# Attention steps between the gate and branch products of the merge, and merged tiles in two of four weight buffers

## What is computed

```python
hn = rms_norm(x, norm_mix[l])
proj = jnp.einsum('bsd,dn->bsn', hn, w_in[l])
p_rwkv, p_pool, p_att, p_gate = jnp.split(proj, split_at, axis=-1)
...
y_a, v_first = rwkv7_bidir(p_rwkv, hn, vres, v_first, ...)
y_b = multiscale_pool(p_pool, pool_w[l], pool_scale[l])
y_c = gqa_axial(p_att, q_norm[l], k_norm[l])
gates = jax.nn.sigmoid(p_gate).reshape(B, S, N_BRANCH, D)
merged = (gates[:, :, 0] * (y_a @ w_branch_rwkv[l]) + gates[:, :, 1] * (y_b @ w_branch_pool[l])
          + gates[:, :, 2] * (y_c @ w_branch_attn[l]))
x = x + merged @ w_out[l]
x = x + expert_choice_ffn(rms_norm(x, norm_ffn[l]), router[l], exp_gate[l], exp_up[l], exp_down[l])
```

## Time and profile before

| | us |
|---|---|
| median of 3 runs | 3319.7 |
| lowest and highest run | 3315.34, 3321.82 |
| span of the profiled execution, first to last instruction | 3318.4 |
| TensorE busy in it | 3219.3 (97%) |
| VectorE busy | 1527.3 (46%) |
| ScalarE busy | 1068.0 (32%) |
| GpSimd busy | 308.7 (9%) |

### The profile page before, as it was taken

One profiled execution on the slowest core, in us unless ns is written; L12 is line 12 of the kernel. 1 busy time (PEld: TensorE's weight loads), 2 busy tenths in 40 slices (PEclk: granted clock), 3 DMA queues, 4 the chain that ended last, 5 costly groups with the idle time before them and its releaser, 6 DMA issues. The chain is left out here.

```text
span 3318.4 us, 46903 instructions
## 1 busy us (share of the span) xinstructions
PE 3219.3 (97%) x20286; PEld 2468.8 (74%) x20286; DVE 1527.3 (46%) x2217; ACT 1068.0 (32%) x1596; POOL 308.7 (9%) x365
## 2 busy tenths in 40 slices
PE   9999999999999999999999999979999999989988
PEld 7888887888888888889788888758877888434332
DVE  5443556644435544332754434685567544201112
ACT  4222226432224322222732223553344323200001
POOL 1000131200001000000300001211111301100000
PEclk9999999999999999999999999989999999999999
DMA  4222441122233222332222222301010323899998
GB/s 144 102 90 90 145 143 40 39 102 89 90 96 113 102 89 90 96 107 108 84 97 94 98 88 98 106 20 49 3 65 20 105 99 124 345 427 425 425 427 336
DMA packets 62799, 448.77 MB, mean 135 GB/s; under 512 B 8705, under 2 KB 10369, under 8 KB 32641
## 3 DMA queue, kind: packets, MB, share of 16 engines
q1 hardware_dynamic: 62592, 445.76, 35.9%
HBM read 438.39 MB, written 2.10 MB: 133 GB/s over the span
## 5 line engine op out<-in xcount | busy, mean ns | idle before, releaser
L569 DVE TENSOR_TENSOR w_lo<-slot,w_hi 128x2048 fp32r<-128x2048 f32 (+4 forms) x243 | 487.1, 2005 | 331.6 <-ACT w_hi L560 329.3
L167 PE MATMUL bank<-xa,w_hi 128*128 128x512 f32 x1368 | 535.9, 392 | 1.2 <-DVE w_lo L3170 1.1
L168 PE MATMUL bank<-xa,w_hi 128*128 128x512 f32 x1368 | 532.4, 389 | 0.0
L169 PE MATMUL bank<-xa,w_lo 128*128 128x512 f32 x1368 | 532.3, 389 | 0.0
L560 ACT ACTIVATE w_hi<-slot 128x2048 fp32r<-128x2048 f32 (+4 forms) x243 | 406.1, 1671 | 335.5 <-PE bank L169 326.3
L167 PE MATMUL bank<-xb,w_hi 128*128 128x512 f32 x832 | 324.7, 390 | 0.7 <-DVE w_lo L569 0.6
L168 PE MATMUL bank<-xb,w_hi 128*128 128x512 f32 x832 | 323.7, 389 | 0.0
L169 PE MATMUL bank<-xb,w_lo 128*128 128x512 f32 x832 | 323.7, 389 | 0.0
L167 PEld LDWEIGHTS bank<-xa,w_hi 128*128 128x128 f32 x1368 | 256.8, 188 | 63.1 <-issue 5.4
L169 PEld LDWEIGHTS bank<-xa,w_lo 128*128 128x128 f32 x1368 | 256.8, 188 | 53.8
L168 PEld LDWEIGHTS bank<-xa,w_hi 128*128 128x128 f32 x1368 | 256.8, 188 | 53.4 <-issue 1.2
(11 more groups left out here) (511 smaller groups left out, 4872.4 us busy)
## 6 DMA issues: line engine op xcount, KB each, us to landing
slot<-in_w_gu SPq DMA_DIRECT2D x87, 1024.0 KB, 4.7
slot<-in_exp_gate SPq DMA_DIRECT2D x25, 2048.0 KB, 15.2
slot<-in_exp_up SPq DMA_DIRECT2D x24, 2048.0 KB, 15.0
slot<-in_exp_down SPq DMA_DIRECT2D x24, 2048.0 KB, 15.8
slot<-in_w_dn SPq DMA_DIRECT2D x64, 704.0 KB, 4.0
slot<-in_w_gate SPq DMA_DIRECT2D x24, 768.0 KB, 4.3
xe<-in_exp_up SPq DMA_DIRECT2D x8, 2048.0 KB, 13.4
xe<-in_exp_down SPq DMA_DIRECT2D x8, 2048.0 KB, 15.2
```

The costliest lines, as they stand in the source:

```text
L167: e.matmul(out, w[0], x[0], start=(j == 0), stop=False)
L168: e.matmul(out, w[0], x[1], start=False, stop=False)
L169: return e.matmul(out, w[1], x[0], start=False, stop=(j == n - 1))
L569: dve.e.tensor_tensor(lo, slot(k, b), hi.bitcast(F32), ALU.subtract).then_inc(L.up("w_lo", b))
```

## The change

The attention of stage `ax` no longer runs ahead of the merge. `pe_attention`, `act_attention` and `dve_attention` take a function `between(t)` that is called at the end of each step, and the merge hands them 20 pieces, one for each step (`AX_PIECES`): the gate and the branch product of the first branch for all 8 tiles in turn, then gate (0, 1), the pool mix, branch (0, 1) and gate (0, 2). The other products come after the attention (`AX_REST`). The weight blocks are reordered to match: first the 8 blocks of branch 0, then tile by tile those of branches 1 and 2. The split of `y_rwkv` into `yr` moves ahead of the attention. ScalarE and VectorE take up a piece one step after TensorE, and split a weight block in every second step.

Memory: `yr` now lies where the attention doesn't use memory; six of the eight tiles `mg` lie in buffers 2 and 3, so that all weights of the merge and of the output product go through buffers 0 and 1, and the first expert block (buffers 2 and 3) waits for the last split tile, `("mg_lo", 7)`.

```diff
+    late_mg = Arena(k.nc, SBUF_END - SLOT - 1024, a.made)
+    m.mg = [late_mg.buf(512, "mg") for _ in range(6)] + [k.sq[1], k.sqsum]
...
-    add("w2_gate", [ins["w2_gate"][m, z] for m in range(KT) for z in range(3)], 1536)
+    add("w2_gate", [ins["w2_gate"][m, 0] for m in range(KT)] + [ins["w2_gate"][m, z] for m in range(KT) for z in (1, 2)], 1536)
...
-        if b == k.first["w2_gate"] + 6:
-            slots = [2] + slots
+        if b == k.first["w2_gate"]:
+            slots.remove(3)
+        if b == k.first["exp"]:
+            slots = [2, 3] + sorted(slots)
+            held[2] = held[3] = ("mg_lo", 7)
...
+AX_PIECES = [(kind, i, 0) for i in range(KT) for kind in ("gate", "branch")] + [("gate", 0, 1), ("mix", 0, 1), ("branch", 0, 1), ("gate", 0, 2)]
+AX_REST = [("branch", 0, 2)] + [(kind, i, z) for i in range(1, KT) for z in (1, 2) for kind in ("gate", "branch")]
...
+    def between(t):
+        if t < len(AX_PIECES):
+            piece(*AX_PIECES[t])
+
+    pe_attention(k, "ax", k.ax.att, ax_units(k), between)
+    for name in AX_REST:
+        piece(*name)
     pe_out(k, "mg", nx, k.first["w2_out"], m.out, lambda i: ("mg_lo", i))
...
+    def between(t):
+        if 0 < t <= len(AX_PIECES):
+            kind, i, z = AX_PIECES[t - 1]
+            if kind == "gate":
+                sigmoid(i, z)
+            if kind == "mix":
+                act_pool_mix(k)
+        if t < 18 and t % 2 == 0:
+            act_weight(k, k.first["w2_gate"] + t // 2 + 1)
+        if t == 19:
+            act_weight(k, gate_block(k, 1, 1))
+
+    act.wait_ge(*L.at("rwkv_out", 3))
+    act.wait_ge(*L.at("z_mean", 3))
     for j in range(4):
         e.activation(m.yr[j][0], col(k.y_rwkv, j), ACT.Copy).then_inc(L.up("yr_hi", j))
+    act_attention(k, "ax", k.ax.att, ax_units(k), between)
```

More of the change, by code:

```diff
@@ L386, in plan_memory @@
     assert b.at <= first_dead.at
-    b = first_dead.copy()
-    late_mg = [b.buf(512, "mg") for _ in range(4)]
+    b = Arena(k.nc, first_dead.at + 2048, a.made)
+    yr_hi, yr_lo = b.copy(), z.copy()
+    m.yr = [(yr_hi.buf(512, "yr", F32R), yr_lo.buf(512, "yr", F32R)) for _ in range(4)]
     k.y_pool = [b.pair("y_pool") for _ in range(4)]
-    m.yr = [b.pair("yr") for _ in range(4)]
-    m.mg = [b.buf(512, "mg") for _ in range(4)] + late_mg
+    late_mg = Arena(k.nc, SBUF_END - SLOT - 1024, a.made)
+    m.mg = [late_mg.buf(512, "mg") for _ in range(6)] + [k.sq[1], k.sqsum]
+    b.at = first_dead.at + 12288
     m.out = [(b.buf(512, "mg_out", F32R), Arena(k.nc, rstd8_at, a.made).buf(512, "mg_out", F32R))] + k.xs[1:]
@@ L856, in width, with pe_attention @@
     return math.prod(keys.shape[1:])
-def pe_attention(k, st, m, units):
+def pe_attention(k, st, m, units, between=None):
     pe, e, L = k.pe, k.pe.e, k.led
@@ L910, in pe_attention, with act_attention @@
                 last.then_inc(L.up("scores", st, t, z))
-def act_attention(k, st, m, units):
+        if between:
+            between(t)
+def act_attention(k, st, m, units, between=None):
     act, e, L = k.act, k.act.e, k.led
@@ L956, in pool_attention, with dve_attention @@
         pool.e.tensor_tensor(out[1], m.ot[s % 3], out[0].bitcast(F32), ALU.subtract).then_inc(L.up("att_out", st, s))
-def dve_attention(k, st, m, units):
+def dve_attention(k, st, m, units, between=None):
     dve, e, L = k.dve, k.dve.e, k.led
@@ L1645, in pe_post @@
     pe_values(k, "ax", 0, k.first["w2_attv"], 128, k.xs, tok)
-    pe_attention(k, "ax", x.att, ax_units(k))
 def by_chunks(b, soon):
@@ L1781, in act_post @@
             L.up("v_out", "ax", 0, i))
-    act.wait_ge(*L.at("rwkv_out", 3))
-    act_attention(k, "ax", x.att, ax_units(k))
 def dve_shift(k, n):
@@ L2016, in dve_post @@
     dve_weight(k, b["w2_gate"])
-    dve_attention(k, "ax", x.att, ax_units(k))
 def pool_rwkv(k):
@@ L2545, in sp_ax, with gate_block, gate_turn @@
         c += n
+def gate_block(k, i, z):
+    return k.first["w2_gate"] + (KT + 2 * i + z - 1 if z else i)
+def gate_turn(i, z):
+    return KT + 2 * i + z - 1 if z else i
+AX_PIECES = [(kind, i, 0) for i in range(KT) for kind in ("gate", "branch")] + [("gate", 0, 1), ("mix", 0, 1), ("branch", 0, 1), ("gate", 0, 2)]
+AX_REST = [("branch", 0, 2)] + [(kind, i, z) for i in range(1, KT) for z in (1, 2) for kind in ("gate", "branch")]
 def pe_merge(k, nx):
@@ L2550, in pe_merge, with piece @@
     ys = [(m.yr, lambda j: ("yr_lo", j)), (k.y_pool, lambda j: ("ypool_lo", j)), (k.y_att, lambda j: ("att_out", "ax", 4 * j + 3))]
[L2551 to L2554, removed]
+    def piece(kind, i, z):
+        if kind == "mix":
+            pe_pool_mix(k)
+            return
+        b = gate_block(k, i, z)
+        w = views(part(k, b), "p (k c) -> p k c", k=12)
+        if kind == "gate":
             pe.wait_ge(*L.at("w_lo", b))
@@ L2560, in pe_merge @@
             last.then_inc(L.up("gate2", i, z))
-            if i == z == 0:
-                pe_pool_mix(k)
+        else:
             bank, freed = k.banks.take(("branch", i, z), ("branch_gated", i, z))
@@ L2574, in act_merge, with sigmoid @@
     act, e, L, m = k.act, k.act.e, k.led, k.mg
-    act.wait_ge(*L.at("att_out", "ax", 15))
+    def sigmoid(i, z):
+        sg = m.sgs[gate_turn(i, z) % 3]
+        act.wait_ge(*L.at("gate2_scaled", i, z))
+        e.activation(sg, sg, ACT.Sigmoid).then_inc(L.up("gate2_sigmoid", i, z))
+    def between(t):
+        if 0 < t <= len(AX_PIECES):
+            kind, i, z = AX_PIECES[t - 1]
+            if kind == "gate":
+                sigmoid(i, z)
+            if kind == "mix":
+                act_pool_mix(k)
[5 more added lines that the diff above has]
+    act.wait_ge(*L.at("z_mean", 3))
     for j in range(4):
         e.activation(m.yr[j][0], col(k.y_rwkv, j), ACT.Copy).then_inc(L.up("yr_hi", j))
[L2578 to L2585, removed]
+    act_attention(k, "ax", k.ax.att, ax_units(k), between)
+    for i in range(1, KT):
+        for z in (1, 2):
+            act_weight(k, gate_block(k, i, z) + 1)
+            sigmoid(i, z)
         if i == 3:
@@ L2597, in dve_merge @@
     dve, e, L, m = k.dve, k.dve.e, k.led, k.mg
-    for j in range(4):
-        dve.wait_ge(*L.at("yr_hi", j))
-        e.tensor_tensor(m.yr[j][1], col(k.y_rwkv, j), m.yr[j][0].bitcast(F32), ALU.subtract).then_inc(L.up("yr_lo", j))
     def split(i):
@@ L2603, in split, with scaled @@
         e.tensor_tensor(m.out[i][1], m.mg[i], m.out[i][0].bitcast(F32), ALU.subtract).then_inc(L.up("mg_lo", i))
[L2605 to L2614, removed]
-                dve_pool_mix(k)
-            if t == 3 * KT - 1:
+    def scaled(i, z):
+        t = gate_turn(i, z)
+        dve.wait_ge(*L.at("gate2", i, z))
+        if t >= 3:
+            n = t - 3
+            dve.wait_ge(*(L.at("branch_gated", n, 0) if n < KT else L.at("merge_add", (n - KT) // 2, (n - KT) % 2 + 1)))
+        e.tensor_tensor(m.sgs[t % 3], k.banks.of("gate2", i, z)[:, :], k.rstd, ALU.mult).then_inc(L.up("gate2_scaled", i, z))
@@ new lines, in gated @@
+    def gated(i, z):
+        sg = m.sgs[gate_turn(i, z) % 3]
+        dve.wait_ge(*L.at("gate2_sigmoid", i, z))
+        dve.wait_ge(*L.at("branch", i, z))
+        e.tensor_tensor(sg if z else m.mg[i], sg, k.banks.of("branch", i, z)[:, :], ALU.mult).then_inc(L.up("branch_gated", i, z))
+        if z:
+            dve.wait_ge(*L.at("branch_gated", i, z))
+            dve.wait_ge(*(L.at("merge_add", i, 1) if z == 2 else L.at("branch_gated", i, 0)))
+            e.tensor_tensor(m.mg[i], m.mg[i], sg, ALU.add).then_inc(
+                L.up("merge_add", i, z, also=[("merged", i)] if z == 2 else []))
@@ new lines, in between @@
+    def between(t):
+        if t == 0:
+            for j in range(4):
+                dve.wait_ge(*L.at("yr_hi", j))
+                y = col(k.y_rwkv, j)
+                e.tensor_tensor(m.yr[j][1], y, m.yr[j][0].bitcast(F32), ALU.subtract).then_inc(L.up("yr_lo", j))
+        if 0 < t <= len(AX_PIECES):
+            kind, i, z = AX_PIECES[t - 1]
+            if kind == "mix":
+                dve_pool_mix(k)
+            else:
+                (scaled if kind == "gate" else gated)(i, z)
+        if t < 18 and t % 2 == 0:
+            dve_weight(k, k.first["w2_gate"] + t // 2 + 1)
+        if t == 19:
+            dve_weight(k, gate_block(k, 1, 1))
@@ L2617, in dve_merge @@
+    dve_attention(k, "ax", k.ax.att, ax_units(k), between)
+    gated(0, 2)
+    for i in range(1, KT):
+        for z in (1, 2):
+            dve_weight(k, gate_block(k, i, z) + 1)
+            scaled(i, z)
+            if (i, z) == (7, 2):
                 for j in (1, 2, 3):
                     split(j)
-            dve.wait_ge(*L.at("gate2_sigmoid", i, z))
-            dve.wait_ge(*L.at("branch", i, z))
-            e.tensor_tensor(sg if z else m.mg[i], sg, k.banks.of("branch", i, z)[:, :], ALU.mult).then_inc(L.up("branch_gated", i, z))
@@ L2622, in dve_merge @@
[L2622 to L2627, removed]
+            gated(i, z)
         if i == 4:
```

## The result

The changed kernel takes 3328.6 us (median of 6 runs, 3326.3 to 3330.6), the kernel before 3317.5 (6 runs, 3315.3 to 3321.8): a ratio of 1.0034, with a 95% interval of 1.0024 to 1.0044. It is slower by 11.1 us. Timed once more, beside an experiment, it took 3328.3 us, ratio 1.0037 (1.0024 to 1.0051). The profiled execution has a span of 3326.0 us, 7.6 above the one before. The two numbers don't contradict each other, as the next paragraphs show.

What follows compares the result with a forecast made beforehand. TensorE's work in attention and merge was taken as the bound, shifting the DMA-fed expert stage one to one. Terms -1.3 + 8.0 + 2.1 = +8.8 us on 3319.7 gave 3328.5 us, range 3319 to 3335.

Steps and rivals of the forecast that it cites:

- Part 1, the start: First attention steps: inserted products fill TensorE's two waits for ScalarE's exponentials, 0.75 and 0.52 us; -1.3 us.
- Part 2, the table loads: Attention: loads of the exponential's table on ScalarE delay freeing a PSUM bank, stalling TensorE 1.34 us in six steps; +8.0 us.
- those six: Attention steps 5, 7, 9, 11, 13 and 15, with both a table load and six banks; 1.34 us each.
- Part 3, the joints: Switches between attention matmuls and inserted products: 0.11 us on each of 19 entries, nothing on leaving; +2.1 us.
- Part 4, two buffers: Merge and output product weights through two buffers, merged tiles in the others: no block late; 0 us.
- The drain: Rival: ScalarE drains fully at each table switch, 1.4 us more in six places; 3336.8 us, chance 0.05.
- The covered loads: Rival: ScalarE's table loads in the attention are covered and the 1.34 us stalls vanish; 3320.5 us, chance 0.13.
- The unpacked attention: Rival: attention really waits for VectorE's copy of the probabilities, so inserted products give 12 us back; 3316.3 us, chance 0.08.
- No gate step stalls: Rival denied here: gate steps stall too, or VectorE is slow beside GpSimd; 3 to 8 us more, chance 0.08.

Runs made afterwards that it cites:

- The kernel with two pieces and the mix first: Changed kernel with tanh gates, only the first gate and branch product inside the attention, pool mix moved ahead of gate (0, 1): 3317.0 us, ratio 1.0002 to before.
- the tanh kernel: Changed kernel with its gates made by tanh instead of the sigmoid, so no table loads in attention and merge: 3318.7 us, ratio 1.0008 to before.
- the sigmoid a gate later: Changed kernel with each gate's sigmoid run inside the next gate product, the exponential's table loaded right behind it: 3319.6 us, ratio 1.0008 to before.

## Why the prediction was right

The forecast was 3328.5 us, the time is 3328.6, and the verdict, slower by more than 0.2%, was the likeliest one. By the stretch, which holds nothing else, the sum of +8.8 stands against +10.6 measured. The forecast started from 3319.7 us, the median of 3 runs, where more runs give 3317.3 to 3317.5: 2.2 too high at the start and 1.8 too low in the sum. The two cancel, so it is luck that the forecast is only 0.1 us off; the mechanism is right and one term is too small. Point by point:

**Part 1, the start, -1.3: right.** No idle time stands ahead of the first transposes or of any scores in the kernel after. The kernel with two pieces and the mix first shows it by itself: -0.7 net, which is -1.27 with two joints (+0.46) and one step that is 0.14 longer.

**Part 2, the table loads, +8.0: right, by steps and by size.** The steps were those six, and the place was the bank. Tanh takes away 8.02 us, 1.34 for each wait as worked out; TensorE's row shows 1.28 of it as idle time. The exponentials' sum was expected 1.96 + 1.41 = 3.37 us after the first transpose; it comes after 3.38 (2576.78 to 2580.16). A pair of steps was expected at about 16.3 us and lasts 16.61, which is the tanh kernel's 15.26 (2562.34 to 2577.60) and 1.35; the 0.3 above the expectation are joints.

**Part 3, the joints, +2.1: the term that was mis-sized.** In the tanh kernel, where nothing else is left, they are 2.56 + 1.27 = 3.8 us, a mean of 0.19 for each of the 20 pieces. The step that failed is "on leaving, the last one is followed after 0.23: nothing". It was read from a product followed by the mix (2574.45 to 2574.68), whose matmuls are of the product's own shape. A product followed by the attention's matmuls with `probsT` takes 0.32 (2573.96 to 2574.28), 0.09 more. Entering costs about what was forecast: ahead of a gate product the scores are followed after 1.08 instead of 1.06 and its first matmul after 0.31 instead of 0.23, 0.10 in all. These rows don't hold the whole of a piece: the tanh kernel's pair of steps, 15.26 us, is 0.45 above two attention steps and 36 matmuls (2 x 3.32 + 36 x 0.227 = 14.81), 0.22 for each piece. The mean is lower because the three pieces that stand behind transposes near the end cost next to nothing. The range given for the term, -4 to +4, held it.

**Part 4, two buffers, 0: right,** shown by itself. No gate product waits for `w_lo`, and the transfers still land in 4.4 us.

**The drain.** The Trainium skill (ScalarE: Activation LUTs, What ACT_TABLE_LOAD costs) would add 1.38 us at each switch. The rows show the next instruction 0.02 us behind a load wherever it doesn't wait for another engine (2578.09 + 1.28 to 2579.39), and at 16.3 us for the term the stretch would have been some 317 us. So the measurement decides: no drain shows here.

**The rivals.** The covered loads would have left no wait; there are six. The unpacked attention would have given 12 us back; the tanh kernel, without any stall, is still 2.6 us above before, and the waits of the weight loads, 8.3 us in the earlier trace rows, were no time of TensorE's. No gate step stalls.

## What to carry to other kernels

Where two curves with different tables are put in turn on ScalarE, look where each load stands: in this kernel 15 more loads in ScalarE's waiting time cost 0.04 us, six in another place 8.0. What has to be looked for is the one instruction behind a load whose result somebody takes up at once, here through a PSUM bank, not through data; any of three edits (a function from the same table, the sigmoid a gate later, a bank that something else frees) took the 8 us away. And this interleaving could only win the idle time that TensorE had (1.27 us), while the changes between products and short matmuls had their price (3.8 us).

## What the runs showed of the hardware

- Between 128 x 512 matmuls of a product and the attention's matmuls of other shapes, a piece put between costs 0.22 us of TensorE in the steady part of the tanh kernel, with no idle time recorded. The last matmul of a product is followed after 0.32 us instead of 0.23 and the first after 0.31. It hangs on the neighbour: a product put behind transposes starts 0.17 us sooner than scores put there (0.85 and 1.02 us behind the first transpose).
- A table load takes 1.28 us, with 0.02 us to the next instruction where that one doesn't wait, both on the path (six times in the kernel after) and off it (with the sigmoid a gate later).
- Programs that are equal up to a point reach it up to 3.4 us apart (2511.39 to 2514.80 for the attention's first matmul). Differences of a few us are read from distances inside the trace.
